# A two-block transformer forward pass on one core: early norms, a shorter forget-gate chain, and a last norm that starts tile by tile

## Chip, cores and metric

One core of one Trainium2 chip runs the whole forward pass. The metric is the device time of an execution in microseconds (us). Lower is better.

## What is computed

Two models run one after the other on one sequence of 512 tokens with 1024 channels. The parts that the change touches are these:

```python
def first_block(x, ...):
    for layer in range(2):
        h = rmsnorm(x, norm_mix[layer])
        x = x + (even_mixer if layer % 2 == 0 else odd_mixer)(h, ...)
        x = x + squared_relu_mlp(rmsnorm(x, norm_mlp[layer]), w_up[layer], w_down[layer])
    return rmsnorm(x, norm_final)

def even_mixer(h, w_in, b_forget, rel_bias, w_out):
    qa, ka, va, fa, qb, kb, vb = _split(h @ w_in, SPLIT_AB)        # fa: 8 columns, one per head
    log_f = jax.nn.log_sigmoid((fa + b_forget).astype(jnp.float32))
    o_a = fox_attention(qa, ka, va, log_f)      # scores + cumsum(log_f)[q] - cumsum(log_f)[k], causal
    o_b = chunked_relpos_attention(qb, kb, vb, rel_bias)
    return jnp.concatenate([o_a, o_b], -1) @ w_out

def second_block(x, ...):
    u = rms_norm(x, attn_norm_g)
    h = x + ((mg[0] * (y_a @ w_branch_a) + mg[1] * (y_b @ w_branch_b)) @ w_out)
    h = h + (jax.nn.silu(u2 @ w_gate) * (u2 @ w_up)) @ w_down      # u2 = rms_norm(h, ffn_norm_g)
    return rms_norm(h, final_norm_g)
```

## The kernel before

Activations lie transposed: channels on the 128 partitions, the 512 tokens along the free axis, so `x` is 8 tiles of 128x512. Every weight comes as a slab of 128x1024 floats (eight 128x128 tiles). A product keeps close to float32 by being three products: each operand is split into a rounded part (`hi`) and the rest (`lo`), and TensorE (PE) adds hi·hi, hi·lo and lo·hi (`product`, L458 to L467), 24 matmuls of 128x512 for a slab. ScalarE (ACT) rounds a slab in two halves (`split`, L1033), GpSimd (POOL) subtracts to get its low part (L440), and SyncE (SP) loads the next slab (L425) when a slot is free. There are two slots of raw, high and low weights and two or three PSUM banks for results; VectorE (DVE) takes results out and signals `gemm_free`.

Each engine has its own program, in an order written out by hand. Semaphores tie them together. An engine that waits holds back all that stands behind it. Four places matter here.

**The start.** ACT loads half of `x`, then for each tile j writes `h_hi` (L1064: x times the norm's gain, rounded) and the square of x (L1051, in two buffers `sq`). DVE writes `h_lo` (L1531) and adds the square to `acc` (L1524), tile by tile, in turn. PE, for each tile, makes three products of 8 columns for the forget gates (L497) and then three products of the first slab, v of pair 0. After tile 7, PE sums the squares over partitions with a matrix of ones (`norm_sum`, L489), DVE makes the mean, ACT makes 1/sqrt by Ln and Exp (`rsqrt`, L1058 and L1059), and only then can results be scaled.

**The gate chain.** With the scale known, DVE scales the 8 rows of forget logits (L1711), ACT makes ln(1+exp(-|z|)) (L1172 to L1174), and DVE adds, scans, splits into high and low, places the parts at four partition ranges of `turned`, and multiplies by four one-hot columns into `fox_b`, four tiles of 128x512 (L1714 to L1727). Behind these on DVE stand the low parts of q and k of pair 0 (L1639). Step 0 of the 32 attention steps (`scores`, L571 and L577) needs them all. Between them PE works on further slabs (`products`), 30 tiles ahead of step 0.

**The merge.** For the eight output tiles of the second model's mixer, DVE makes `m_hi` and `m_lo` (L2151 to L2153). The output projection (`project_out`, eight slabs) starts with one wait for all eight:

```python
            pe.wait_ge(act_lo, c.lo.at(8))
            c.lo.now += 8
            project_out(m_hi, m_lo)
```

**The end.** The last slab's result is added to x (L1569), squared (L1051), added to `acc` (L1524), summed by PE (L489), turned into a mean by DVE (L1561) and into `rstd` by ACT (L1058, L1059). Then DVE multiplies tile by tile by gain and rstd (L1539), and ACT issues one store of 256 KB after each (L1476).

## Time and profile before

| | |
|---|---|
| median of 3 runs | 2142.93 us (2142.56 to 2143.94) |
| the profiled execution | 2140.77 us |
| its span, first to last instruction | 2139.0 us |
| mean granted TensorE clock | 0.985 of full speed |
| busy: PE / DVE / ACT / POOL | 95% / 47% / 42% / 41% |
| HBM traffic | 83 GB/s over the span |

Read it as a kernel in which PE is busy nearly all the time, so that time is lost where PE stands still or runs at the lower clock, and at the two ends, where PE has nothing to do yet or any more. Starts are in us from the span's start. A matmul's listed duration contains its pipeline; what one costs in a row of them is the distance between two starts.

### The profile page before, as it was taken

How to read it: one execution, taken by the hardware profiler on the slowest of the kernel's cores; microseconds unless marked ns; L12 is line 12 of the kernel's file. 1: busy time of each engine (PE TensorE's matmuls, PEld its weight loads, DVE VectorE, ACT ScalarE, POOL GpSimd, SP SyncE). 2: the span in 40 equal slices, each digit the busy share in tenths (PEclk: the TensorE clock that was granted, in tenths of full speed). 3: DMA queues.
4: the chain of work that ended last, by engine and by line, in shares of the span. 5: the costliest groups of instructions: out<-in, count | busy, mean ns of one | idle time of the engine just before them, and what ended most of it. 6: DMA issues, size and time to landing. Idle time of an engine off the chain costs nothing. (4 is left out here: it accounts for less than half of the span.)

```text
span 2139.0 us, 28743 instructions
## 1 busy us (share of the span) xinstructions
PE 2036.3 (95%) x9992; PEld 1614.6 (75%) x9992; DVE 999.0 (47%) x1603; ACT 908.8 (42%) x1773; POOL 871.6 (41%) x648
## 2 busy tenths in 40 slices
PE   7999999999999978899999998998999999999997
PEld 5777688888887755688888886766667878888885
DVE  6445545322355677542312265777564553323134
ACT  4555543333343664442323355655554233223233
POOL 3223345444454221244444453542113545545454
PEclk9999999999999999999999999999999999999998
DMA  4222122222222110122222221321112222232223
GB/s 142 71 70 79 60 98 96 93 97 98 98 99 80 59 40 30 41 97 92 97 98 98 98 92 66 99 89 41 39 40 69 96 82 92 96 99 99 99 95 103
DMA packets 50614, 177.89 MB, mean 83 GB/s; under 512 B 5568, under 2 KB 5832, under 8 KB 50512
## 3 DMA queue, kind: packets, MB, share of 16 engines
q1 hardware_dynamic: 47536, 171.02, 24.2%
q10 hardware_dynamic: 2976, 5.48, 0.8%
q8 instruction: 68, 1.11, 0.2%
q14 instruction: 34, 0.28, 0.0%
HBM read 174.36 MB, written 2.12 MB: 83 GB/s over the span
## 5 line engine op out<-in xcount | busy, mean ns | idle before, releaser
L440 POOL TENSOR_TENSOR w_lo<-raw,w_hi 128x512 fp32r<-128x512 f32 x644 | 871.4, 1375 | 1247.9 <-ACT w_hi L1033 1247.7
L1033 ACT ACTIVATE w_hi<-raw 128x512 fp32r<-128x512 f32 x644 | 371.0, 624 | 844.4 <-PE gemm_banks L467 826.3
L465 PE MATMUL gemm_banks<-h_hi,w_hi 128*128 128x512 f32 x1512 | 614.6, 406 | 7.0 <-POOL w_lo L440 6.8
L467 PE MATMUL gemm_banks<-h_hi,w_lo 128*128 128x512 f32 x1512 | 593.4, 392 | 0.0
L466 PE MATMUL gemm_banks<-h_lo,w_hi 128*128 128x512 f32 x1512 | 593.1, 392 | 0.0
L465 PEld LDWEIGHTS gemm_banks<-h_hi,w_hi 128*128 128x128 f32 x1512 | 284.9, 188 | 89.3 <-issue 28.4
L465 PE MATMUL gemm_banks<-u_hi,w_hi 128*128 128x512 f32 x848 | 330.5, 390 | 4.2 <-POOL w_lo L440 2.9
L467 PEld LDWEIGHTS gemm_banks<-h_hi,w_lo 128*128 128x128 f32 x1512 | 284.8, 188 | 62.4
L466 PE MATMUL gemm_banks<-u_lo,w_hi 128*128 128x512 f32 x848 | 330.1, 389 | 0.0
L467 PE MATMUL gemm_banks<-u_hi,w_lo 128*128 128x512 f32 x848 | 330.1, 389 | 0.0
L466 PEld LDWEIGHTS gemm_banks<-h_lo,w_hi 128*128 128x128 f32 x1512 | 285.4, 189 | 57.0 <-issue 2.6
L1569 DVE TENSOR_TENSOR x<-gemm_banks,x 128x512 f32<-128x512 f32 x112 | 77.4, 691 | 316.8 <-PE gemm_banks L467 314.7
L465 PEld LDWEIGHTS gemm_banks<-u_hi,w_hi 128*128 128x128 f32 x848 | 159.2, 188 | 38.9 <-issue 3.7
L467 PEld LDWEIGHTS gemm_banks<-u_hi,w_lo 128*128 128x128 f32 x848 | 159.2, 188 | 33.1
L466 PEld LDWEIGHTS gemm_banks<-u_lo,w_hi 128*128 128x128 f32 x848 | 159.3, 188 | 32.8
L1770 DVE TENSOR_TENSOR u_lo<-tmp,u_hi 128x512 fp32r<-128x512 f32 x86 | 108.7, 1264 | 126.0 <-ACT u_hi L1224 109.0
L1142 ACT ACTIVATE probs<-score_banks,top 128x128 f32<-128x128 f32 (+3 forms) x192 | 99.4, 523 | 133.5 <-DVE top L1672 122.0
L1150 ACT ACTIVATE probs<-probs,share 128x128 f32<-128x128 f32 (+3 forms) x160 | 81.1, 554 | 75.1 <-DVE share L1694 36.6
L1505 DVE TENSOR_TENSOR tmp<-gemm_banks,rstd 128x512 f32<-128x512 f32 x52 | 36.0, 692 | 147.2 <-PE gemm_banks L467 145.9
L1762 DVE SCALAR_TENSOR_TENSOR tmp<-gemm_banks,rstd 128x512 f32<-128x512 f32 x64 | 44.3, 692 | 120.8 <-PE gemm_banks L467 118.0
L1524 DVE TENSOR_TENSOR acc<-acc,sq 128x512 f32<-128x512 f32 x59 | 78.6, 1333 | 10.8 <-ACT sq L1051 10.1
L1672 DVE CUSTOM_DVE_ANT_0 score_banks<-score_banks,sin 128x128 f32<-128x128 f32 (+3 forms) x96 | 45.3, 514 | 36.2 <-PE score_banks L920 36.1
(307 smaller groups left out, 1943.3 us busy)
## 6 DMA issues: line engine op xcount, KB each, us to landing
raw<-slabs SPq DMA_DIRECT2D x322, 512.0 KB, 3.2
table<-rel_rows ACTq DMA_DIRECT2D x4, 512.0 KB, 3.9
y_t<-x ACTq DMA_DIRECT2D x8, 256.0 KB, 2.1
x<-x_t SPq DMA_DIRECT2D x4, 256.0 KB, 6.6
x<-x_t ACTq DMA_DIRECT2D x4, 256.0 KB, 7.2
cos<-pos SPq DMA_DIRECT2D x2, 256.0 KB, 9.5
consts<-consts_packed SPq DMA_DIRECT2D x1, 452.5 KB, 8.2
params<-params_packed ACTq DMA_DIRECT2D x1, 211.5 KB, 4.3
```

The costliest lines, as they stand in the source:

```text
L440: pool.tensor_tensor(w_lo[:, j, part], raw[:, j, part], w_hi[:, j, part].bitcast(F32), ALU.subtract).then_inc(slab_split, 1)
L465: pe.matmul(out, high, rhs_hi, start=first, stop=False)
L466: pe.matmul(out, high, rhs_lo, start=False, stop=False)
L467: return pe.matmul(out, low, rhs_hi, start=False, stop=last)
L1033: act.activation(w_hi[:, m % 2, part], raw[:, m % 2, part], ACT.Copy).then_inc(slab_hi, 1)
L1142: act.activation(probs[:, b, head, 0:w], SC[:, 2 * b + head, 0:w], ACT.Exp, bias=top[:, b, head:head + 1], scale=-1.0, accum_out=mass[:, b ...
L1150: act.activation(probs[:, b, head, 0:w], probs[:, b, head, 0:w], ACT.Copy, scale=share[:, b, head:head + 1]).then_inc(evened, 1)
L1524: dve.tensor_tensor(sums[:, :], sums[:, :], sq[:, c.acc.slot, :], ALU.add).then_inc(acc_ready, 1)
L1569: dve.tensor_tensor(x[:, j, :], bank, x[:, j, :], ALU.add).then_inc(gemm_free, 1)
L1672: last = dve.tensor_tensor_reduce(z, z, masks[head], -1.0, 3e38, ALU.add, ALU.min, top[:, b, head:head + 1])
L1762: dve.scalar_tensor_tensor(tmp[:, s, :], result(), 0.0, rstd[:, :], ALU.max, ALU.mult).then_inc(gemm_free, 1)
L1770: dve.tensor_tensor(u_lo[:, j, :], tmp[:, 2 + s, :], u_hi[:, j, :].bitcast(F32), ALU.subtract).then_inc(act_lo, 1)
```

## The change

The squares of the input go into eight tiles of `g_b` (idle at that time), one each, and ACT makes all eight `h_hi` first. PE runs five products of zeros while it waits for the first tile. The forget gates take two products for a tile of x, not three: one with 40 columns (8 high, 24 zero, 8 low) and one with 8, all after the first slab. The sum of squares is asked of PE two tiles into the next slab. The gate chain is shorter: sigma is made from a Relu and the Ln, the scan takes both, ones times one-hot (128x128) replaces the four wide `fox_b`, and the mask and the one-hot tiles are made ahead of the scan. V of pair 0 is turned during k, not q. The lambda, bias-row and identity tables move into attention steps 0 to 2. The output projection's first slab waits tile by tile. At the end, the sum of squares is made in two parts, ACT reads the sum from PSUM, x times gain is made beside the slabs, DVE multiplies in six pieces, and SP and ACT issue a store each in turn.

```diff
@@ units
-                if (name == "q" and j == TURN_AT) or (name == "q1" and j == 1):
+                if (name == ("q" if p else "k") and j == TURN_AT and n == KT) or (name == "q1" and j == 1):
                     yield "vt", p, 0, 0
...
+FINAL = [(0, 1), (1, 2), (2, 4), (4, 6), (6, 7), (7, 8)]
@@ sync
+            for n in range(0, len(FINAL), 2):
+                sp.wait_ge(y_ready, n + 1)
+                sp.dma_start(y_rows(y_out, n), x[:, slice(*FINAL[n]), :]).then_inc(y_stored, 16)
@@ tensor
-            pe.wait_ge(forget_split, 2)
+            pe.wait_ge(zeros_ready, 1)
+            for n in range(5):
+                pe.matmul(SC[:, 0, :], turned[:, 0, 0:P], turned[:, 0, :], start=True, stop=True)
             for kt in range(KT):
                 pe.wait_ge(act_lo, c.lo.at(kt + 1))
-                for n, (w, h) in enumerate(((wf_hi, h_hi), (wf_hi, h_lo), (wf_lo, h_hi))):
-                    last = pe.matmul(OB[0:8, :], w[:, kt, :], h[:, kt, :], start=(kt == 0 and n == 0), ...
...
+            for kt in range(KT):
+                pe.matmul(OB[0:40, :], wf[:, kt, :], h_hi[:, kt, :], start=kt == 0, stop=False, ...
+                last = pe.matmul(OB[0:8, :], wf[:, kt, 0:8], h_lo[:, kt, :], start=False, stop=kt == KT - 1, ...
             pe.wait_ge(small_landed, 16)
-            norm_sum(KT, bank=0)
...
-            products(KT, AB_AHEAD)
+            products(KT, KT + 2)
+            norm_sum(KT, bank=0)
+            products(KT + 2, AB_AHEAD)
...
-            pe.wait_ge(act_lo, c.lo.at(8))
-            c.lo.now += 8
-            project_out(m_hi, m_lo)
+            gemm_slab(m_hi, m_lo, fresh=1)
+            for n in range(1, KT):
+                gemm_slab(m_hi, m_lo)
...
-            norm_sum(KT)
+            pe.wait_ge(acc_ready, c.acc.at(KT - 1))
+            pe.matmul(OB[:, :], ones, acc[:, :], start=True, stop=False)
+            pe.wait_ge(sq_ready, c.acc.at(KT))
+            pe.matmul(OB[:, :], ones, sq[:, (c.acc.now + KT - 1) % 2, :], start=False, stop=True).then_inc(norm_full, 1)
@@ scalar
                 gained(j, gains_of("mix0"))
-                square(x[:, j, :])
-                if j == 5:
+            for j in range(KT):
+                if j == 4:
                     split(1)
+                act.activation(g_b[:, j, :], x[:, j, :], ACT.Square).then_inc(sq_ready, 1)
...
             products(0, KT)
+            rsqrt(rstd)
...
+            act.activation(tmp[0:8, 3, :], tmp[0:8, 2, :], ACT.Relu, bias=small[0:8, 4:5], scale=-1.0)
...
+            products(KT, 2 * KT)
+            act.wait_ge(fox_ready, 5)
+            act.activation(fox[64:72, :], tmp[0:8, 2, :], ACT.Copy).then_inc(fox_hi, 1)
...
                     if finish:
                         act.wait_ge(gemm_free, c.gemm.at())
                         square(x[:, j, :])
+                        act.activation(g_b[:, j, :], x[:, j, :], ACT.Copy,
+                                       scale=gains_of("final2")[:, j:j + 1]).then_inc(gained_out, 1)
...
-            rsqrt(rstd)
+            link(act.activation(rstd[:, :], OB[:, :], ACT.Ln, bias=small[:, 5:6], scale=1.0 / D))
+            act.activation(rstd[:, :], rstd[:, :], ACT.Exp, scale=-0.5).then_inc(rstd_ready, 1)
@@ vector
-            mean(D, rstd)
-            g = PC["final2"].start
-            for j in range(KT):
-                normed(x[:, j, :], params[:, g + j:g + j + 1], x[:, j, :], rstd)
+            dve.wait_ge(rstd_ready, c.rstd.at(1))
+            dve.wait_ge(gained_out, KT)
+            for low, high in FINAL:
+                dve.tensor_tensor(x[:, low:high, :], g_b[:, low:high, :],
+                                  rstd[:, :].unsqueeze(1).to_broadcast([P, high - low, S]), ALU.mult).then_inc(y_ready, 1)
```

How the order moves, at the three places the prediction speaks of. First PE at the start of the program, before (`wf` are the forget weights, `out_bank` their PSUM bank):

```order
L497 MATMUL out_bank<-h_hi,wf_hi 8x512 [waits act_lo,forget_split]
L497 MATMUL out_bank<-h_lo,wf_hi 8x512
L497 MATMUL out_bank<-h_hi,wf_lo 8x512
L465 MATMUL gemm_banks<-h_hi,w_hi 128x512 [waits slab_split]
L466 MATMUL gemm_banks<-h_lo,w_hi 128x512
L467 MATMUL gemm_banks<-h_hi,w_lo 128x512
```

and now:

```order
L512 MATMUL score_banks<-turned 128x512 [waits zeros_ready]
L512 MATMUL score_banks<-turned 128x512 x4
L482 MATMUL gemm_banks<-h_hi,w_hi 128x512 [waits slab_split,act_lo]
L483 MATMUL gemm_banks<-h_lo,w_hi 128x512
L484 MATMUL gemm_banks<-h_hi,w_lo 128x512
L482 MATMUL gemm_banks<-h_hi,w_hi 128x512 [waits act_lo]
```

The forget products have gone from between the tiles and stand, two for a tile, behind the slab's 24 products. The five products of zeros wait for a memset only.

Second, DVE from the last `h_lo` to the scan and the low parts of q and k, before:

```order
L1531 SCALAR_TENSOR_TENSOR h_lo<-x,params,h_hi 128x512 [waits act_hi]
L1524 TENSOR_TENSOR acc<-acc,sq 128x512 [waits acc_ready,sq_ready]
L1619 TENSOR_SCALAR ident_r<-consts 128x128 [waits small_landed]
```

and now:

```order
L1574 SCALAR_TENSOR_TENSOR h_lo<-x,params,h_hi 128x512 [waits act_hi] x8
L1669 TENSOR_TENSOR acc<-g_b 128x512 [waits sq_ready]
L1669 TENSOR_TENSOR acc<-acc,g_b 128x512 [waits acc_ready,sq_ready] x6
L1673 COPY tmp<-out_bank 8x512 [waits forget_full]
L1674 TENSOR_TENSOR tmp<-tmp,out_bank 8x512 [waits dve_step]
L1604 TENSOR_SCALAR rstd<-score_banks 128x512 [waits norm_full,dve_step]
L1752 TENSOR_TENSOR tmp<-tmp,rstd 8x512 [waits rstd_ready]
```

All eight `h_lo` now come ahead of all seven additions, and the tables (three masks, lambda) that stood between the additions and the mean are gone from here; `PE` asks for the sum of squares after 6 products of the next slab.

Third, PE at the output projection, before:

```order
L465 MATMUL gemm_banks<-m_hi,w_hi 128x512 [waits slab_split,gemm_free,act_lo]
L466 MATMUL gemm_banks<-m_lo,w_hi 128x512
L467 MATMUL gemm_banks<-m_hi,w_lo 128x512
L465 MATMUL gemm_banks<-m_hi,w_hi 128x512
L466 MATMUL gemm_banks<-m_lo,w_hi 128x512
```

and now:

```order
L482 MATMUL gemm_banks<-m_hi,w_hi 128x512 [waits act_lo,slab_split,gemm_free]
L483 MATMUL gemm_banks<-m_lo,w_hi 128x512
L484 MATMUL gemm_banks<-m_hi,w_lo 128x512
L482 MATMUL gemm_banks<-m_hi,w_hi 128x512 [waits act_lo]
L483 MATMUL gemm_banks<-m_lo,w_hi 128x512
```

The products stand where they stood; each of the eight tiles now waits for its own `act_lo`, where the first waited for the count of all eight.

## Rows read from the trace of the kernel before

**Rows 1.** PE's waits over the whole span: total us, times, longest
```profile
PE gemm_banks L465 <- POOL w_lo L440: 9.8, 5, 4.3
PE out_bank L497 <- DVE h_lo L1531: 8.9, 1, 8.9
PE score_banks L571 <- DVE k_lo L1639: 4.9, 1, 4.9
PE gemm_banks L465 <- DVE m_lo L2153: 4.7, 1, 4.7
```
**Rows 2.** Timeline, PE at the start and at the first sum of squares
```profile
10.16 0.63 PE L465 MATMUL gemm_banks<-h_hi,w_hi 128*128 128x512 f32 x1
...
14.23 0.39 PE L497 MATMUL out_bank<-h_lo,wf_hi 128*8 128x512 f32 x1
14.46 0.39 PE L497 MATMUL out_bank<-h_hi,wf_lo 128*8 128x512 f32 x1
...
22.23 1.02 PE L489 MATMUL score_banks<-acc,consts 128*128 128x512 f32 x2
```
**Rows 3.** Timeline, ACT and DVE, first input tiles
```profile
6.50 0.72 ACT L1064 ACTIVATE h_hi<-x,params 128x512 fp32r<-128x512 f32 x1 [0.32 <-DMA x<-x_t]
7.13 0.61 ACT L1051 ACTIVATE sq<-x 128x512 f32<-128x512 f32 x1
...
7.26 1.52 DVE L1531 SCALAR_TENSOR_TENSOR h_lo<-x,params,h_hi 128x512 fp32r<-128x512 f32 x1 [1.61 <-ACT h_hi L1064]
```
**Rows 4.** Timeline, DVE and POOL meeting in SBUF
```profile
14.76 0.69 DVE L1524 TENSOR_TENSOR acc<-acc,sq 128x512 f32<-128x512 f32 x1
15.36 1.79 DVE L1531 SCALAR_TENSOR_TENSOR h_lo<-x,params,h_hi 128x512 fp32r<-128x512 f32 x1
...
14.17 4.13 POOL L440 TENSOR_TENSOR w_lo<-raw,w_hi 128x512 fp32r<-128x512 f32 x2 [5.94 <-ACT w_hi L1033]
25.98 2.53 POOL L440 TENSOR_TENSOR w_lo<-raw,w_hi 128x512 fp32r<-128x512 f32 x2 [7.69 <-ACT w_hi L1033]
```
**Rows 5.** Timeline, PE at attention step 0 and after it
```profile
43.62 0.48 PE L571 MATMUL score_banks<-fox_b,ones_r 64*128 64x128 f32 x2 [4.90 <-DVE k_lo L1639]
...
44.67 0.79 PE L465 MATMUL gemm_banks<-h_hi,w_hi 128*128 128x512 f32 x1
...
48.20 0.40 PE L467 MATMUL gemm_banks<-h_hi,w_lo 128*128 128x512 f32 x1
```
**Rows 6.** Timeline, PE, DVE and POOL at the output projection
```profile
1711.67 2.93 POOL L440 TENSOR_TENSOR w_lo<-raw,w_hi 128x512 fp32r<-128x512 f32 x2 [2.89 <-ACT w_hi L1033]
...
1714.92 0.69 DVE L2153 TENSOR_TENSOR m_lo<-tmp,m_hi 128x512 fp32r<-128x512 f32 x1
1715.67 0.80 PE L465 MATMUL gemm_banks<-m_hi,w_hi 128*128 128x512 f32 x1 [4.74 <-DVE m_lo L2153]
...
1720.83 0.40 PE L465 MATMUL gemm_banks<-m_hi,w_hi 128*128 128x512 f32 x1
1721.06 0.40 PE L466 MATMUL gemm_banks<-m_lo,w_hi 128*128 128x512 f32 x1
```
**Rows 7.** Timeline, the last norm and the stores
```profile
2124.97 0.63 ACT L1051 ACTIVATE sq<-x 128x512 f32<-128x512 f32 x1 [3.45 <-DVE x L1569]
...
2126.43 1.70 PE L489 MATMUL out_bank<-acc,consts 128*128 128x512 f32 x2 [2.23 <-DVE acc L1524]
2128.17 0.69 DVE L1561 TENSOR_SCALAR rstd<-out_bank 128x512 f32<-128x512 f32 x1 [1.79 <-PE out_bank L489]
...
2130.22 6.26 DVE L1539 SCALAR_TENSOR_TENSOR x<-x,params,rstd 128x512 f32<-128x512 f32 x8 [1.36 <-ACT rstd L1059]
2131.00 5.85 ACTq L1476 DMA_DIRECT2D y_t<-x  x8
```
**Rows 8.** Stretches of 1 us: PEclk, DMA share and GB/s are the last three
```profile
10.00:11.00 1.00, 1.00 (x3) 0.73 (x3) 1.00 (x3) 1.00 (x3) 0.00 (x0) 1.00 1.07 428
...
2133.00:2134.00 1.00, 0.00 (x0) 0.00 (x0) 0.96 (x2) 0.00 (x0) 0.00 (x0) 0.50 0.94 344
```

More of the change, by code:

```diff
@@ L273, in e_valued, with y_rows @@
     return 128 + (s if s <= DIFF_STEPS else 2 * s - DIFF_STEPS)
+FINAL = [(0, 1), (1, 2), (2, 4), (4, 6), (6, 7), (7, 8)]
+def y_rows(y_out, n):
+    low, high = FINAL[n]
+    return y_out[low * P:high * P, :].rearrange("(j p) s -> p j s", p=P)
 def build(nc, slabs, x_in, params_in, consts_in, pos1_in, pos2_in, rel_in, lam_in, y_out):
@@ L507, in _ @@
             c.lo.now += KT
+            pe.wait_ge(forget_split, 3)
+            for kt in range(KT):
+                pe.matmul(OB[0:40, :], wf[:, kt, :], h_hi[:, kt, :], start=kt == 0, stop=False, skip_group_check=True)
+                last = pe.matmul(OB[0:8, :], wf[:, kt, 0:8], h_lo[:, kt, :], start=False, stop=kt == KT - 1,
+                                 skip_group_check=True)
+            last.then_inc(forget_full, 1)
             pe.wait_ge(small_landed, 16)
-            norm_sum(KT, bank=0)
-            pe.wait_ge(masks_ready, 3)
             used, done = {}, {}
@@ L1113, in _ @@
                 gained(j, gains_of("mix0"))
-                square(x[:, j, :])
-                if j == 5:
+            for j in range(KT):
+                if j == 4:
                     split(1)
-            act.wait_ge(lam_in_ready, 1)
-            act.activation(small[:, 2:4], small[:, 0:2], ACT.Exp).then_inc(lam_exp, 1)
-            rsqrt(rstd)
+                act.activation(g_b[:, j, :], x[:, j, :], ACT.Square).then_inc(sq_ready, 1)
+            c.acc.now += KT
             def products(low, high):
@@ L1187, in _ @@
                 products(*half(s, 1))
+                if s == 1:
+                    act.wait_ge(lam_in_ready, 1)
+                    act.activation(small[:, 2:4], small[:, 0:2], ACT.Exp).then_inc(lam_exp, 1)
+                    act.wait_ge(rel_ready, 3)
+                    act.dma_start(rel_rows, table[0:8, 1, :, :].rearrange("p a b -> p (a b)")[:, 0:E_LEN]).then_inc(
+                        rel_stored, 16)
             mixed(7)
@@ L1564, in mean, with add_out @@
                 c.rstd.now += 1
-            def add_out(gains=None, beside=lambda j: None, more=False, squares=True):
+            def add_out(gains=None, beside=lambda j: None, more=False, squares=True, last_apart=False):
                 for j in range(KT):
@@ L1572, in add_out @@
                         gained(j, gains)
-                    if squares:
+                    if squares and (j < KT - 1 or not last_apart):
                         add_square(j == 0)
@@ L1620, in _ @@
-            dve.tensor_tensor(gain2[:, :], gains_of("final1"), gains_of("attn2"), ALU.mult)
-            lam = VT[:, 0:256].rearrange("p (a b d) -> p a b d", a=2, b=2)
-            dve.wait_ge(pos_landed, 48)
-            prods = VT[:, 256:384].rearrange("p (a d) -> p a d", a=2)
-            link(dve.tensor_tensor(prods, lam[:, :, 0, :], lam[:, :, 1, :], ALU.mult))
-            dve.tensor_reduce(small[:, 0:2], prods, X, ALU.add).then_inc(lam_in_ready, 1)
-            dve.wait_ge(lam_exp, 1)
-            link(dve.scalar_tensor_tensor(neg_lam[:, :], small[:, 3:4], -LAM_INIT, small[:, 2:3], ALU.add,
-                                          ALU.subtract))
+            for j in range(1, KT):
+                dve.wait_ge(sq_ready, j + 1)
+                if j > 1:
+                    dve.wait_ge(acc_ready, j)
+                dve.tensor_tensor(acc[:, :], (acc if j > 1 else g_b[:, 0, :])[:, :], g_b[:, j, :],
+                                  ALU.add).then_inc(acc_ready, 2 if j == 1 else 1)
@@ L1632, in _ @@
+            c.acc.now += KT
+            dve.wait_ge(forget_full, 1)
+            link(dve.tensor_copy(tmp[0:8, 3, :], OB[32:40, :]))
+            link(dve.tensor_tensor(tmp[0:8, 2, :], tmp[0:8, 3, :], OB[0:8, :], ALU.add))
             mean(D, rstd, 0)
@@ L1754, in _ @@
                 bias_table(s)
+                if s == 0:
+                    tables_begun()
+                if s == 2:
+                    dve.wait_ge(lam_exp, 1)
+                    dve.scalar_tensor_tensor(neg_lam[:, :], small[:, 3:4], -LAM_INIT, small[:, 2:3], ALU.add, ALU.subtract)
+                    for name, tile in (("ident", ident_r), ("strict", strict_r)):
+                        dve.tensor_scalar(tile[:, :], consts[:, CO[name]], 1.0, None, ALU.mult).then_inc(masks_ready, 1)
+                    dve.tensor_tensor(gain2[:, :], gains_of("final1"), gains_of("attn2"), ALU.mult)
             mixed(7)
```

110 lines of the change are left out of this document (59 added, 51 removed).

## The prediction

> **What bounds the kernel now.** The page's first part says PE is busy 95% of the span, so I read PE's waits next. Nearly all of them are short waits in the attention stages, which the change leaves alone. Three are touched: 8.9 us before the first product, 4.9 us ahead of attention step 0, and 4.7 us ahead of the output projection [rows 1]. The fourth place is the end, where PE is done and a chain of single operations and stores runs [rows 7]. The largest sum in the list, POOL's 9.8 us in five waits [rows 1], is at other slabs; the first of them in time lies far behind step 0, and no edit reaches it.
>
> A wait costs more than its length. Behind the wait of 4.74 us, 12 products of 128x512 take 5.16 us (1715.67 to 1720.83), 0.43 us each, and then they stand 0.23 us apart [rows 6]: the clock at 1.2 and at 2.4 GHz. The same two paces are seen at the start, where a product's listed 0.63 us becomes 0.39 and the distance 0.23 (14.23 to 14.46) [rows 2], and behind the wait of 4.9 us, up to about 48 us [rows 5].
>
> **The start.** Before, PE does 48 products and one sum between 8.9 and 22.7, and starts step 0 at 43.62 [rows 2, 5]. I put the new program through the rows' durations.
>
> - PE: five float32 products of zeros from about 1.5 us. One of these, in two passes, costs 1.70 us at the low clock [rows 7] and about 0.9 at the high one (its two passes are listed with 1.02, of which the last 0.1 or so overlaps with what follows) [rows 2]. Two and a half slow, the rest fast: done near 8, ahead of the first tile. So they cost nothing, and leave PE at 2.4 GHz when tile 0 comes.
> - Tile 0's `h_lo` ends at 8.78, as before [rows 3]. ACT's `h_hi` now follow each other at some 0.62 us (start of L1064 to start of L1051, 6.50 to 7.13), so DVE sends tiles faster than PE takes them (3 x 0.23 = 0.69 us). The slab ends at 8.85 + 8 x 0.69 = 14.4; the 16 forget products make it 14.4 + 16 x 0.23 = 18.1. Before, slab and forget products ended at 22.2. That is 4.1 us won so far, 1.8 of it from 8 products fewer, and 2.3 from the clock and the pace.
> - Then 6 products, to 19.4, and PE wants the squares' sum. Here the change gives back. DVE adds only after the last `h_lo`, from 13.1 us, and that is when POOL takes two slabs in a row (ACT rounds slab 1 from about 13.6 and slab 2 from about 16.8). Where both work on SBUF, a DVE operation of 0.69 takes 1.79 and POOL's pair 4.13 and not 2.53 [rows 4]: they go one at a time, in turn. Seven additions alone are 7 x 0.62 = 4.3 us, so 17.5; in turn with four POOL operations of 1.25 I get 21 to 22.3. PE waits 2 to 3 us. The clock may drop once more here (it was down after 2.23 us of idling at the end [rows 7]).
> - From the sum at 22.3: 0.9, then 18 products of q (4.1), 24 of k and the turning of V (6.0), 6 of v1 x 3 ahead of step 0 (4.1): PE arrives at 37.4. DVE's chain for step 0 is beside that: mean and rsqrt to 25.8, scaled logits 26.5, four ACT operations to 29.2, the scan to 30.6, and then what is late now is the pair of fox low parts and k_lo, which again meet POOL's next slab: 38 to 38.7. I take **38.0**.
>
> Gain at step 0: 43.6 - 38.0 = 5.6. The wait there shrinks from 4.9 to about 1 us, so the slow stretch behind it goes: 44.67 to 48.20 for 8 distances [rows 5] is 3.5 us where 8 x 0.23 = 1.8, and the eight small score products before it lose half of 1.05: 2.1 us. The start brings **7.7 us**, between 5 (a second drop of the clock at 19.4) and 10 (the additions slip between POOL's operations, step 0 at 36).
>
> The tables moved into steps 0 to 2 are a dozen small operations, under 2 us of DVE in all and one ACT issue, in stretches where both wait for PE. Cost 0; without that cover, at most 2 us. Relu, the copy of 8 rows and the negated bias are in the chain above.
>
> **The output projection.** `m_lo` of tile 7 ends at 1715.6 whatever PE does [rows 6]. PE is free at 1710.8 (4.74 us before 1715.67). Tiles 0 to 6 are 21 products at the 0.233 us of this stage (1720.83 to 1721.06) [rows 6], 4.9 us: PE reaches tile 7 at 1715.7, just when it is there. Won: 4.9 us of waiting, and the 12 slow products, 1715.67 to 1720.83 = 5.16 us for 12 x 0.233 = 2.8, so 2.4. Together **7.2 us**. What comes next is slab 1, asked for at 1716.4; POOL has it at 1714.6 [rows 6]. Bounds 6.5 and 7.4.
>
> **The end.** Before: square ends 2125.6, addition, sum 2126.43 to 2128.1 at the low clock, mean, Ln, Exp, first multiply at 2130.22, first store issued at 2131.00 [rows 7]. Now the sum over seven squares is done while x is added and squared, so PE's gap is 0.7 us and not 2.2, and I expect the high clock: last square 2125.6, sum 2126.5, Ln and Exp (1.36 from the mean's end to the first multiply, with hand-overs) 2127.9, first piece 2128.6, issue 2128.7. That is 2.3 us sooner (addition 0.7, mean 0.7, clock 0.8, the rest hand-overs). The product with the gain on ACT (0.72 for a tile) has 2 to 3 us of idling before it, and the last one ends before the sum does.
>
> Will the stores keep up? Eight stores go out 0.79 us apart [rows 7], and the 16 DMA engines are 94% busy at 344 GB/s [rows 8]. So they, not DVE, nearly set the pace already; DVE's pieces at about 0.6 us a tile only fill the last 6%: 2.1 MB at 365 GB/s instead of 344 is 0.35 us. At the start both queues together moved 428 GB/s [rows 8], though reading HBM. If two issuing queues brought that rate here, 2.1 MB would take 4.9 us for 6.1, 1.2 us won and not 0.35. I take 0.35, since this row is of the same direction. The Trainium skill (DMA: Bandwidth & Descriptors, on issuing engines and queues) says that SP and ACT queues share the same 16 engines and a second one saves issue time only; by it the sum stays at 0.35, and no run so far shows stores on two queues. The end brings **2.7 us**, between 1.5 (the sum at the low clock) and 4.
>
> **The sum.** 7.7 + 7.2 + 2.7 = 17.6 us. On the profiled execution's 2140.77 that is 2123.2; its time is 2.2 below the median of the runs, 2142.93, and the forecast is for a median: **2125.3 us**. The three places are in line on PE, so their gains add. A measurement of this kernel can tell some 0.2% (4.3 us) from no change.
>
> **Rivals.**
>
> - *The additions slip through* (chance 0.14). POOL let two DVE operations in a row pass before at 14 us [rows 4]. With the squares done by 20 us PE hardly waits, step 0 starts at 36, and with full DMA rate at the end the sum is 10 + 7.3 + 3.7 = 21: 2122. Against it: four POOL operations now fall into the seven additions.
> - *The clock* (0.18). The products of zeros end early, or the wait for the squares drops the clock again. Eight tiles at 0.43 us a product would end the slab 3 to 4 us later, of which the wait for the squares hides most; a drop at 19.4 costs up to 12 slow products, 2.3 us; the sum at the end at the low clock 0.8. Then 5 + 7.2 + 1.6 = 13.8: 2129. For it: the same 4.7 us wait and the 2.2 us one both ended in a slow stretch. The Trainium skill (TensorE: Matmul & The Clock Gate, Part 1) says that the number of slow products at a start varies from run to run; by that rule this case and the forecast may alternate between runs of one kernel. The runs before differ by 1.4 us in all.
> - *The projection's tile waits do nothing* (0.04): were the first product to wait for all eight tiles still, as the order of semaphore counts could make it, 7.2 us are missing: 2132.5. The order shows separate waits, so this is small.
> - *Slower* (0.01). The clock, once up on products of zeros and idle again, stays low through the first attention steps. Each product of 128x512 at 1.2 GHz costs 0.2 us more [rows 2], so 17.6 us are used up after 88 such products, and 110 (13 tiles of 8 short) would give 2147. The trace speaks against it: the slow stretches behind both waits ended, the longer after 12 products [rows 5, 6].
>
> The rest, 0.63, is my forecast, with 2122.5 to 2128 as its own range.
>
> **How the numbers follow.** The range should reach the first two rivals: from 2121 to 2130 only the projection's failure and worse are outside. Faster by over 0.2% needs under 2138.6: all cases but the last, 0.97. Within 0.2%: 0.02. Slower: 0.01.
>
> **What would show it.** Step by step: PE's first slab product at about 8.9 with 0.23 us distances; a wait of 2 to 3 us for `acc` near 19.4; step 0 at 38; no wait ahead of the projection, and its tile 7 within 0.3 us of `m_lo`; the last sum in about 0.9 us, the first store near 2128.7 less 15 (about 2114), and a DMA share near 1 behind it. The forecast is wrong if the first slab's products stand 0.42 us apart, if step 0's wait for k_lo stays at several us, or if a wait of over 1 us appears in attention steps 0 to 3, where the tables went.

## The result, and the profile after

| | before | after |
|---|---|---|
| median of the runs, us | 2143.24 (5 runs) | 2131.32 (5 runs, 2129.74 to 2131.77) |
| profiled execution, us | 2140.77 | 2129.74 |
| its span, us | 2139.0 | 2127.9 |

The ratio of after to before is 0.9948, 95% interval 0.9937 to 0.9959: 11.1 us faster by the ratio, 11.9 by the medians. The forecast was 2125.3 us, with a range of 2121 to 2130. The time lies outside the range, 6.0 us above the forecast: of 17.6 us expected, 11.9 came (11.0 between the two profiled executions). Lines of the kernel after stand 17 to 43 further down: the three products are now L482 to L484, POOL's subtraction L457, `norm_sum` L506, the scores L592 and L598.

**The three places.** First the start. The timeline of PE in the kernel after (start us, duration, engine, line, operation, tiles, and in brackets the idle time ahead of it and what ended it):

```profile
1.46 7.50 PE L512 MATMUL score_banks<-turned 128*128 128x512 f32 x10 [1.46 <-DVE turned L1650]
8.79 0.50 PE L482 MATMUL gemm_banks<-h_hi,w_hi 128*128 128x512 f32 x1
...
14.41 0.39 PE L526 MATMUL out_bank<-h_hi,wf 128*40 128x512 f32 x1
...
17.87 0.39 PE L527 MATMUL out_bank<-h_lo,wf 128*8 128x512 f32 x1
...
22.44 1.13 PE L506 MATMUL score_banks<-acc,consts 128*128 128x512 f32 x2 [2.79 <-DVE acc L1669]
```

and DVE and POOL beside it:

```profile
14.08 8.30 DVE L1669 TENSOR_TENSOR acc<-acc,g_b 128x512 f32<-128x512 f32 x6
...
14.69 3.00 POOL L457 TENSOR_TENSOR w_lo<-raw,w_hi 128x512 fp32r<-128x512 f32 x2 [6.49 <-ACT w_hi L1061]
18.46 3.38 POOL L457 TENSOR_TENSOR w_lo<-raw,w_hi 128x512 fp32r<-128x512 f32 x2 [0.77 <-ACT w_hi L1061]
```

The six additions take 8.30 us, 1.38 each, where the first, ahead of POOL's slabs, took 0.68: the two engines go in turn, as in [rows 4]. PE waits 2.79 us for them. Then step 0, which stood at 43.62 with a wait of 4.90 [rows 5]:

```profile
38.90 0.33 PE L592 MATMUL score_banks<-fox,fox_of 64*128 64x128 f32 x2 [1.23 <-DVE k_lo L1682]
...
39.49 0.50 PE L482 MATMUL gemm_banks<-h_hi,w_hi 128*128 128x512 f32 x1
39.83 0.40 PE L483 MATMUL gemm_banks<-h_lo,w_hi 128*128 128x512 f32 x1
```

At the output projection no wait is left ahead of the first `m_hi` product, where 4.74 us stood [rows 6]. PE reaches tile 7 (1714.04) when its `m_lo` has just been written; the distance behind that product is 0.34 us (1714.04 to 1714.38), the others stay at 0.23:

```profile
1709.08 0.40 PE L482 MATMUL gemm_banks<-m_hi,w_hi 128*128 128x512 f32 x1
...
1714.04 0.50 PE L482 MATMUL gemm_banks<-m_hi,w_hi 128*128 128x512 f32 x1
1714.38 0.39 PE L483 MATMUL gemm_banks<-m_lo,w_hi 128*128 128x512 f32 x1
```

The end, all engines:

```profile
2115.26 1.02 PE L1043 MATMUL out_bank<-acc,consts 128*128 128x512 f32 x2
...
2116.86 1.12 PE L1045 MATMUL out_bank<-sq,consts 128*128 128x512 f32 x2 [0.59 <-ACT sq L1079]
2118.09 0.69 ACT L1514 ACTIVATE rstd<-out_bank,small 128x512 f32<-128x512 f32 x1 [0.66 <-PE out_bank L1045]
...
2119.52 4.77 DVE L2239 TENSOR_TENSOR x<-g_b,rstd 128x512 f32<-128x512 f32 x6 [3.37 <-ACT rstd L1515]
2120.24 3.81 SPq L444 DMA_DIRECT2D y_t<-x  x3
2120.85 3.83 ACTq L1519 DMA_DIRECT2D y_t<-x  x3
```

From the last square to the first store it was 6.03 us (2124.97 to 2131.00) [rows 7]; now it is 2120.24 - 2116.18 = 4.06, with the square starting at 2116.18. Two stretches of 1 us behind that (columns as in [rows 8]) show the store rate late in the tail, about 380 GB/s where 344 stood. Over the whole tail, from the first store's issue to the end of the span, it is 7.7 us (2120.24 to 2127.9) where 8.0 stood (2131.00 to 2139.0):

```profile
2124.00:2125.00 1.00, 0.00 (x0) 0.00 (x0) 0.29 (x1) 0.00 (x0) 0.00 (x0) 0.50 1.02 387
2125.00:2126.00 1.00, 0.00 (x0) 0.00 (x0) 0.00 (x0) 0.00 (x0) 0.00 (x0) 0.50 1.02 383
```

**So where are the missing microseconds?** I laid the two traces side by side: the same instruction on DVE, its start before minus its start after. These are worked out from the two traces, in us (the first column is the time in the kernel before):

```
at 74.89    (attention 1 has settled)     +6.81
at 684.7    (end of the first MLP)        +6.85
at 718                                    +4.8
at 815                                    +5.1
at 871                                    +4.0
at 1316                                   +3.6
at 1564                                   +3.4
at 1577.75  (late in attention 3)         +1.69
at 1723.90  (behind output projection)    +8.78
at 2124.24  (last x)                      +8.79
end of the span                          +11.0
```

The start brought 6.8, the projection 7.1, the end 2.3: 16.2 us. But in attention stages two and three, between 684 and 1578, 5.1 us went again, though the change was meant to leave them alone. The largest groups of PE's waits are nearly what they were. Before (three groups of the attention stages that [rows 1] leaves out, each larger than its 9.8 us):

```profile
PE score_banks L760 <- ACT probs L1292: 15.5, 8, 3.7
PE out_bank L966 <- DVE turned L2087: 13.0, 11, 3.7
PE out_bank L774 <- DVE turned L1879: 11.7, 15, 2.2
```

and after:

```profile
PE score_banks L783 <- ACT probs L1328: 15.5, 8, 3.7
PE out_bank L990 <- DVE turned L2145: 12.7, 11, 3.7
PE out_bank L797 <- DVE turned L1937: 11.1, 13, 2.4
PE gemm_banks L482 <- POOL w_lo L457: 10.1, 6, 4.3
```

One wait did grow, and by the change's own doing. The new condition in `units` (V of pair 0 is turned during k and not q) holds for stage two as well. There too V's turning moved, and DVE now copies V right ahead of what `k_lo` needs. Before:

```profile
676.61 0.69 DVE L1839 COPY V<-gemm_banks 128x512 f32<-128x512 f32 x1
...
688.06 0.33 PE L750 MATMUL score_banks<-k_hi,q_hi 64*128 64x128 f32 x2 [1.68 <-DVE k_lo L1821]
```

and after:

```profile
679.01 0.69 DVE L1897 COPY V<-gemm_banks 128x512 f32<-128x512 f32 x1
...
681.95 0.33 PE L773 MATMUL score_banks<-k_hi,q_hi 64*128 64x128 f32 x2 [2.33 <-DVE k_lo L1879]
```

PE waits 0.65 us longer there. The wait is 2.33 us in all four profiles with the new start and no fill products (those come below), and 1.7 in all four with the old one. So some 0.7 of the 5.1 us is no matter of the clock.

For the rest, what differs is the granted clock. In that stretch, 11 pieces of the trace after are at 0.50, together 54.6 us; in the trace before it was 37.5 us in 7 pieces. All of them start during a wait of PE or just behind one. For instance the one that begins with the wait of 4.3 us for `w_lo` (stretches; PEclk, DMA share and GB/s are the last three):

```profile
1290.00:1294.00 4.00, 1.70 (x8) 1.09 (x6) 2.12 (x4) 1.81 (x4) 0.00 (x0) 1.00 0.00 0
1294.00:1304.00 10.00, 6.53 (x17) 4.88 (x18) 3.84 (x6) 4.68 (x8) 5.01 (x4) 0.51 0.14 52
1304.00:1308.00 4.00, 4.00 (x20) 2.94 (x19) 0.75 (x2) 0.89 (x2) 0.17 (x1) 0.94 0.43 131
```

and its first products, at 0.43 us instead of 0.23:

```profile
1295.98 0.77 PE L482 MATMUL gemm_banks<-h_hi,w_hi 128*128 128x512 f32 x1 [4.28 <-POOL w_lo L457]
1296.55 0.63 PE L483 MATMUL gemm_banks<-h_lo,w_hi 128*128 128x512 f32 x1
1296.97 0.63 PE L484 MATMUL gemm_banks<-h_hi,w_lo 128*128 128x512 f32 x1
```

Theory A: what was lost is TensorE's clock in stages two and three, whose low stretches fall differently in each execution. Theory B: the change itself does something to those stages. Rival C: the low clock there is harmless, because the engine that PE waits for sets the time. (Each expectation below letters its own theories anew.)

### The profile page after: what moved, and what is told of

It is laid out like the page before. It is cut to its first block and busy times, and to the rows that moved or that the text cites. A ratio compares the mean times of both kernels' runs of the same rounds, so it can differ in the third digit from the quotient of the medians.

```text
span 2127.9 us, 28756 instructions
## 1 busy us (share of the span) xinstructions
PE 2043.0 (96%) x9996; PEld 1619.3 (76%) x9996; DVE 999.3 (47%) x1600; ACT 915.1 (43%) x1783; POOL 871.1 (41%) x648
## 5 line engine op out<-in xcount | busy, mean ns | idle before, releaser
L457 POOL TENSOR_TENSOR w_lo<-raw,w_hi 128x512 fp32r<-128x512 f32 x644 | 870.9, 1373 | 1239.7 <-ACT w_hi L1061 1239.5
L482 PE MATMUL gemm_banks<-h_hi,w_hi 128*128 128x512 f32 x1512 | 615.4, 407 | 7.4 <-POOL w_lo L457 7.2
L484 PE MATMUL gemm_banks<-h_hi,w_lo 128*128 128x512 f32 x1512 | 593.7, 393 | 0.0
L482 PEld LDWEIGHTS gemm_banks<-h_hi,w_hi 128*128 128x128 f32 x1512 | 285.1, 189 | 89.6 <-issue 28.2
L482 PE MATMUL gemm_banks<-u_hi,w_hi 128*128 128x512 f32 x848 | 330.3, 390 | 4.1 <-POOL w_lo L457 2.9
L484 PEld LDWEIGHTS gemm_banks<-h_hi,w_lo 128*128 128x128 f32 x1512 | 285.2, 189 | 62.9
L484 PE MATMUL gemm_banks<-u_hi,w_lo 128*128 128x512 f32 x848 | 329.9, 389 | 0.0
L482 PEld LDWEIGHTS gemm_banks<-u_hi,w_hi 128*128 128x128 f32 x848 | 159.2, 188 | 38.8 <-issue 3.7
L484 PEld LDWEIGHTS gemm_banks<-u_hi,w_lo 128*128 128x128 f32 x848 | 159.2, 188 | 33.2
L1567 DVE TENSOR_TENSOR acc<-acc,sq 128x512 f32<-128x512 f32 x51 | 71.0, 1391 | 10.1 <-ACT sq L1079 9.3
```

The lines of the kernel that those rows point to most:

```text
L457: pool.tensor_tensor(w_lo[:, j, part], raw[:, j, part], w_hi[:, j, part].bitcast(F32), ALU.subtract).then_inc(slab_split, 1)
L482: pe.matmul(out, high, rhs_hi, start=first, stop=False)
L484: return pe.matmul(out, low, rhs_hi, start=False, stop=last)
L1567: dve.tensor_tensor(sums[:, :], sums[:, :], sq[:, c.acc.slot, :], ALU.add).then_inc(acc_ready, 1)
```

## The experiments

Medians are of all runs of a kernel; the kernel before ran beside each set, and its median was 2142.51, 2141.97 and 2142.10 in the three.

### Set 1: the change in parts, and each kernel profiled again

**The new start alone.** The change without the projection's tile-wise wait and without the new end:

```diff
-            gemm_slab(m_hi, m_lo, fresh=1)
-            for n in range(1, KT):
-                gemm_slab(m_hi, m_lo)
+            pe.wait_ge(act_lo, c.lo.at(8))
+            c.lo.now += 8
+            project_out(m_hi, m_lo)
...
```

> The changed kernel with the old output projection wait and the old end: only the start and the attention steps 0 to 2 are changed. Theory A (each part is worth what its place shows, and the stages between are as they were): 6.9 us faster than before, as at the end of the first attention stage. Theory B (the part is worth that, but the stages between lose part of it because other waits there end at the lower clock): 1.5 to 4 us faster, and the profile shows more low-clock stretches between 600 and 1700 us than the seven of the kernel before. Theory C (the moved tables or the changed buffers slow the stages themselves): the same loss as B, but with longer waits and the same number of low stretches.

Measured: 2138.71 us (2135.83 to 2143.64, 10 runs), ratio 0.9986 (0.9976 to 0.9995): 3.0 us faster by the ratio, 3.8 by the medians. The executions of this one program lie 7.8 us apart. Its profiled execution had a low stretch that the trace after does not have, behind the wait for `acc`:

```profile
22.65 1.72 PE L492 MATMUL score_banks<-acc,consts 128*128 128x512 f32 x2 [2.75 <-DVE acc L1644]
23.38 1.42 PE L468 MATMUL gemm_banks<-h_hi,w_hi 128*128 128x512 f32 x1
24.60 0.63 PE L469 MATMUL gemm_banks<-h_lo,w_hi 128*128 128x512 f32 x1
```

It cost 2.1 us (the gain at 74.89 is 4.73 and not 6.81), and 5.1 more went in the stages, with 10 low stretches there where the kernel before has 7. That is what its theory B named, time and stretches; the 6.9 us of its theory A did not come.

**Everything but the new start.** The kernel before with the projection and the end of the change:

```diff
-            pe.wait_ge(act_lo, c.lo.at(8))
-            c.lo.now += 8
-            project_out(m_hi, m_lo)
+            gemm_slab(m_hi, m_lo, fresh=1)
+            for n in range(1, KT):
+                gemm_slab(m_hi, m_lo)
...
-            norm_sum(KT)
+            pe.wait_ge(acc_ready, c.acc.at(KT - 1))
+            pe.matmul(OB[:, :], ones, acc[:, :], start=True, stop=False)
...
```

> The kernel before with the tile-by-tile output projection and the new end alone. All that comes ahead of the merge is untouched, so all theories expect the stages between as before, and a gain of 7.1 at the projection and 2.3 at the end: 9.4 us faster. If it is well under 9, the low stretch behind the projection's wait was not there in most executions, and the profile of before overstates it.

Measured: 2131.26 us (2130.63 to 2134.01, 4 runs), ratio 0.9947 (0.993 to 0.9963): 11.3 us faster, more than expected and as fast as the whole change. Its profiled execution, the slowest of the four (2134.01), lost 3.6 us in the stages, with the old start. That speaks against theory B in its simplest form: no new start is needed for such a loss. But this execution is 2.75 us above the median of its kernel, and its stages lost nothing at the two places that go with the new start (the longer wait for `k_lo` above, and one at 1566 that is named further down).

**The two kernels again,** unchanged:

> The changed kernel once more, for a second profile. If the low-clock stretches depend on how the program lies in time to something outside it, they stand at other waits than in the first profile and their number differs by one to four. If they are the program's own, they stand at the same eleven places.

> The kernel before once more, for a second profile: the same question. If the stretches are the program's own: again nine between 40 and 1722 us at the same waits. If not: other places, and a time that differs with their number, about 1 us for each.

Measured: 2130.14 and 2142.07. The second profile of the kernel after lost 5.1 us in the stages once more, with 10 of the 11 low stretches at the same waits; only the one at 1321 is missing. So they are mostly the program's own. The second profile of the kernel before differs from the first by up to 1.6 us in mid-program (+1.54 at 813, -1.45 at 1533). Six of its seven stretches in the stages stand behind the same waits again; the one at 689.8 to 693.3 is missing, and a piece at 868.1 to 871.5 and one at 1325.5 to 1328.9 are new. Same program, same waits, mostly the same stretches, and some that come and go.

### Set 2: the clock held up

> The changed kernel itself, timed again beside the three others of this set. Theory A (each execution lays the stretches of low granted clock in the long middle stages anew, and the kernel after met more of them): median 2129 to 2133, and the stretches near 683, 707, 765, 806, 864, 1294, 1321, 1407, 1479, 1523 and 1567 us come back at about the same places, because the same waits stand ahead of them. Theory B (the 5.1 us that were lost between 684 and 1576 us were an accident of one execution): some executions near 2125 to 2127.

Measured: 2129.27 us (2126.30 to 2130.58, 5 runs), ratio 0.9942 (0.9929 to 0.9956). The profiled execution lost 3.3 us in the stages; low stretches lie near 683, 765, 1294, 1403, 1475, 1519 and 1564 again, one near 792 is new, and those at 707, 806, 864 and 1321 are missing. The places mostly come back, and one execution of five, 2126.30, also lies where the other theory put some: the loss is neither wholly fixed nor a single accident; part of it is drawn anew in each execution.

**Fill products.** Products of zeros ahead of the waits behind which the clock was low, each group shorter than its wait (135 products of 128x512 in all, more than the estimate in the expectation):

```diff
+FILL_CD_FLIP = {2: 6, 6: 5, 10: 12, 11: 3, 13: 4, 14: 7, 15: 7}
+FILL_CD_VALUES = {15: 7, 18: 4, 22: 4, 26: 7}
+FILL_E_SLAB = {("kc", 0): 13, ("k", 1): 6}
+FILL_E_FLIP = {36: 5}
+FILL_E_VALUES = {9: 10, 18: 11, 27: 10, 37: 3}
...
+            def fill(n, to=None):
+                for _ in range(n):
+                    pe.matmul(OB[:, :] if to is None else to, zero_r[:, :], zero_r[:, :].unsqueeze(1)...)
...
                 p, i, b, w = block_of(s)
+                fill(FILL_CD_FLIP.get(s, 0))
                 pe.wait_ge(evened, cd_evened(s))
```

In this form they write zeros over finished columns of the attention output's bank, so later values are others than the reference's; every instruction of the kernel still runs.

> The changed kernel with products of zeros on PE ahead of the fifteen or so waits after which the clock was low (attention stages two and three, about 115 products of 0.227 us = 26 us, each group shorter than the wait that it stands in). Theory A: the clock stays at 2.4 GHz there, the low time of 54 us falls under 20, and since PE's products take 0.43 instead of 0.227 us in it, 4 to 15 us come back: 2116 to 2127. Theory B (the low clock does not matter, because the engine that is waited for sets the time): 2130 to 2133. Theory C (the fill products hold up PE more than the clock gives): over 2133.

Measured: 2119.11 us (2118.10 to 2121.32, 4 runs), ratio 0.9899 (0.9883 to 0.9914): 10.2 us faster than the kernel after beside it (2129.27). Between 684 and 1578 no low stretch is left. This is the number of that expectation's theory A; its B (the low clock does not matter, rival C above) and its C fall.

> The kernel before with the same fill products at the same places. Theory A (the parts of the change add where the clock in the stages between is the same for both): it is slower than the filled changed kernel by 15 to 17 us (6.8 at the start, 7.1 at the projection, 2.3 at the end, as the profiled executions gave them), where the kernels without fill products differ by 11.9. Theory B (what was lost between is not the clock but something that the change does to the stages): the two filled kernels differ by 11 to 13 us again.

Measured: 2131.88 us (2130.77 to 2132.07, 5 runs), ratio 0.9955 (0.9942 to 0.9969): 10.1 us faster than the kernel before. So in the medians the fill products gave both kernels the same, some 10 us. The two filled kernels differ by 12.8 us, 2 to 4 less than theory A expected and inside what B expected. The traces say where it is short: the start of the filled changed kernel again had a low stretch, at 23.6 to 27.0, and had gained 4.7 us at 74.89, not 6.8. The wait for `k_lo` at the start of stage two is still there in it (0.7 us behind the fill products) and not in the filled kernel before, and the projection's wait in the filled kernel before was followed by a shorter low stretch (1706.3 to 1709.7), so that 6.4 us lie between the two there and not 7.1. Only the next set could tell the two theories apart.

```profile
22.71 1.26 PE L519 MATMUL score_banks<-acc,consts 128*128 128x512 f32 x2 [2.75 <-DVE acc L1692]
23.27 1.13 PE L490 MATMUL gemm_banks<-h_hi,w_hi 128*128 128x512 f32 x1
24.20 0.63 PE L491 MATMUL gemm_banks<-h_lo,w_hi 128*128 128x512 f32 x1
```

**The projection alone** (the first diff hunk of the run without the new start, on the kernel before):

> The kernel before with the output projection waiting tile by tile, and nothing else. By the profiled executions the projection gave 7.1 us of its own: 2135 to 2136.5. If the start only re-deals the clock, this part keeps its whole gain, and with the end's 2.3 it explains most of what the run without the new start gained (11.3). Rival (low clock behind the projection's start comes back in another place): under 5 us, 2137.5 or more.

Measured: 2133.72 us (2133.27 to 2136.71, 6 runs), ratio 0.9965 (0.9953 to 0.9977): 7.5 us by the ratio, 8.3 by the medians, 1.3 us better than the expected range. The profiled execution gained 7.05 behind the projection and had lost nothing in the stages (-0.03 at 1577.75); its low stretches there are the seven of the first profile of before, at the same times to 0.4 us.

### Set 3: held clock, and each part undone

The fill products now go only into columns of the bank in which no value stands yet, so nothing is overwritten, and eight more stand in the start:

```diff
+            def fill(n, to=None, low=0):
+                to, open_ = (OB[:, low:S], True) if to is None else (to, False)
+                for _ in range(4 * n * P // (S - low)):
+                    pe.matmul(to, zero_r[:, :], zero_r[:, :].unsqueeze(1).to_broadcast([P, (S - low) // P, P]), ...)
...
             products(KT, KT + 2)
+            pe.wait_ge(zeros_ready, 2)
+            fill(8, SC[:, 0, :])
             norm_sum(KT, bank=0)
```

> The changed kernel with the fill products of the run before (now only into columns of the bank that no value stands in), and eight more of them in the start, ahead of PE's wait for acc, behind which a stretch of low clock lay in two of the profiled executions with the new start (23.0 to 26.5 us in one, 23.6 to 27.0 in the other). Theory A (the clock is what is lost, in the start too): the start keeps its whole gain, against 4.4 at 48 us in the filled run, so 2116 to 2118.5, with no low stretch before the last products. Theory B (the start's loss was something else): 2119 again.

Measured: 2118.07 us (2117.69 to 2119.18, 4 runs), ratio 0.9892 (0.9876 to 0.9909). It leaves nothing out, and beats both kernels: 24.0 us faster than before, 11 to 13 faster than the change. Its page, and the pieces of its timeline that answer to those above:

```profile
PE   9999999999999989999999999999999999999997
...
PEclk9999999999999999999999999999999999999999
```

```profile
19.69 1.99 PE L514 MATMUL score_banks<-zero_r 128*128 128x512 f32 x8
22.67 1.13 PE L521 MATMUL score_banks<-acc,consts 128*128 128x512 f32 x2 [0.99 <-DVE acc L1696]
...
23.86 0.39 PE L491 MATMUL gemm_banks<-h_lo,w_hi 128*128 128x512 f32 x1
...
1287.30 3.13 PE L514 MATMUL gemm_banks<-zero_r 128*128 128x512 f32 x13
1291.64 0.50 PE L490 MATMUL gemm_banks<-h_hi,w_hi 128*128 128x512 f32 x1 [1.21 <-POOL w_lo L465]
1291.98 0.39 PE L491 MATMUL gemm_banks<-h_lo,w_hi 128*128 128x512 f32 x1
```

```profile
1289.00:1299.00 10.00, 6.89 (x32) 5.12 (x31) 4.55 (x7) 4.82 (x8) 5.05 (x4) 1.00 0.16 54
```

The thirteen fill products take 3.13 us of the wait for `w_lo`; `w_lo` lands no sooner, but the products behind it stand 0.23 us apart and not 0.43. The stretch of 10 us is at clock 1.00, where the kernel after had 0.51. The only low stretch left in the trace is the one behind the last products. The fill is not free: groups that may use only 128 or 256 columns of the bank cost more for their columns (28 of 128 columns, as many columns as 7 of 512, take 3.24 us, and the 7 of 512 take 1.77), and likely for that, between 783 and 813 this kernel won 0.7 us where the run before won 1.7.

Now each part of the change is undone in this kernel. First the start (the fill products of the start go with it):

> The run best with the start of the kernel before (its own low stretch at 41 to 48 us is left in). Theory A, gains add when the clock between is held: slower than best by 6.5 to 7.3 us. Rival (the start's gain is given back in the stages whatever the clock does): by under 5.

Measured: 2124.37 us (2123.10 to 2125.55, 4 runs): 6.3 slower than best. In the two traces it is 7.05 us at 74.89 (6.57 and -0.48) and 5.95 at 1577.75: of the 1.1 between, 0.7 is the wait for `k_lo` at the start of stage two, which the old `units` takes away.

Then the projection:

> The run best with the output projection waiting for all tiles at once, as before. Theory A: slower than best by 6.4 to 7.3 us (4.9 of wait and about 2.2 of low clock behind it). Rival: only the wait counts, 4.9 or less, if the clock stays high behind it in most executions.

Measured: 2125.31 us (2124.03 to 2128.63, 4 runs): 7.2 slower.

Then the end:

> The run best with the end of the kernel before (last square in acc, normalisation and stores tile by tile on one queue). Theory A: slower than best by 2.3 to 2.7 us, what the profiled executions and the prediction gave. Rival (the end's gain is larger in the median than in the profiled executions): 3.5 or more.

Measured: 2119.94 us (2119.55 to 2121.25, 4 runs): 1.9 slower.

The projection lies inside what theory A expected, the start 0.2 and the end 0.4 us below it; the rivals of all three (under 5, 4.9 or less, 3.5 or more) fall. Together 15.4 us. For all kernels the gains over the first trace of before, at the same landmarks (us, from one profiled execution each):

```
                  at 74.89  1577.75  1723.90  2124.24  between 74.89 and 1577.75
after                6.81     1.69     8.78     8.79      -5.1
after, again         6.45     1.31     8.42     8.41      -5.1
after, timed again   6.52     3.26    10.35    10.35      -3.3
new start only       4.73    -0.33     0.36     0.34      -5.1
no new start         1.01    -2.62     4.50     4.51      -3.6
projection only      0.11    -0.03     7.05     7.04      -0.1
before, again       -0.61    -1.28    -1.06    -1.05      -0.7
before, filled       0.53     9.77    10.46    10.45      +9.2
after, filled        4.74    13.32    20.41    20.43      +8.6
best                 6.57    13.68    20.50    20.48      +7.1
best, old start     -0.48     7.73    12.97    12.97      +8.2
best, old proj.      6.56    13.82    13.22    13.22      +7.3
best, old end        6.54    13.77    20.65    20.63      +7.2
```

The last column scatters by 5 us in the seven executions without fill products, and by 2 in the six with them. The seven divide by their start. Three of the four with the new start lost 5.1 us and one 3.3; the three with the old start lost 0.1, 0.7 and 3.6. Two places make most of that. One is the wait for `k_lo`, 0.7 us. The other is in late stage three. The product group ahead of it starts after a shorter wait with the new start (0.51 us for 0.79), and PE waits longer at this one; before, and after:

```profile
1569.11 0.88 PE L929 MATMUL score_banks<-consts,probs 128*128 128x128 f32 x6 [1.38 <-ACT probs L1150]
```

```profile
1565.85 0.87 PE L953 MATMUL score_banks<-consts,probs 128*128 128x128 f32 x6 [1.66 <-ACT probs L1175]
```

The wait is 1.66 us in all four with the new start, and a low stretch stands behind it in all four (1567.3 to 1570.7 in the first), which costs 1.6 us in three and 3.2 in the one timed again. It is 1.38 us in all four traces with the old start (the first of before included), and none has a low stretch there or loses anything. Together that is 2.3 us, or 3.9 in the one timed again, that went with the new start each time. What is left, 2.8 us to a gain of 0.6, overlaps with the 0 to 3.6 of the old start, and of that the draw can be the cause.

## Why the prediction was wrong

**What held.** Each place did what the sum said. The products of zeros ended at 8.96, free, and left the clock high; the first slab product came at 8.79 (8.85 expected), the slab ended at 14.4 (14.4), the forget products at 18.1 (18.1). PE waited 2.79 us for `acc` (2 to 3), whose additions went in turn with POOL, and the sum came at 22.44 (22.3). Step 0 came at 38.90 (38.0; 38 to 38.7 was the spread I gave): the fox low parts and `k_lo` stand in DVE's queue until 38.84. The low stretch behind it went, as expected. The tables in steps 0 to 2 cost nothing that shows: no wait of over 1 us there. At the projection 7.2 was expected and 7.1 measured (the sum counts 4.9 us of waiting where its own row has 4.74), by the trace, by the run alone (7.05 in its trace) and by undoing it (7.2). At the end the first store came 2.0 us sooner and the tail behind it was 0.3 shorter, 2.3 for 2.7; the 0.35 for the stores was about right.

**Sizes.** The start was worth 6.8 and not 7.7 (0.9 us, step 0's later start), the end 2.3 and not 2.7. With 0.1 at the projection those are 1.4 of the 6.5 us between the sum (2123.2 for the profiled execution) and its 2129.74.

**The step that failed** is the last one of the sum: "The three places are in line on PE, so their gains add." They are in line, and by the runs at held clock they add: 6.3 + 7.2 + 1.9 = 15.4 with each undone. But I treated the 1500 us between the first two places as a fixed length that is only shifted ("the attention stages, which the change leaves alone"). It is not. PE waits there some 20 times for 1 to 4 us, and behind such a wait the clock may be at 1.2 GHz or not. The first trace of before had 37.5 us of low clock in those stages, the trace after 54.6, and 5.1 us of the missing 6.5 went there. Of these, 0.7 is no clock but the longer wait for `k_lo`, which the change itself made; 1.6 is the low stretch at 1567, which came with the new start in four profiles of four and without it in none of four; the other 2.8 lie within what executions of the old start also lose (0 to 3.6). So the term that the sum put at nothing is the length of the stages between, and it held two things: a loss that goes with the change, and a scatter that a single execution of each kernel cannot show.

The medians say the same. Undone at held clock the parts give 15.4 us (the longer wait for `k_lo` is already in that, since best has it too), and the change gave 11.9 in its medians. So some 3.5 us more were lost to the clock than in the kernel before; a mere draw, the same for both kernels, would hardly show in medians, though those of best and its variants are of 4 runs each.

I had looked at the two waits that the change removes and seen the low clock behind both [rows 5, 6], and priced its going at 2.1 and 2.4 us. The same pricing applied to the other waits of [rows 1] and their neighbours would have shown that the kernel had 37.5 us of slow stretches elsewhere, and that these are a source both of scatter and of gain. But [rows 1] holds only four groups of waits, and the prediction calls POOL's 9.8 us the largest sum in that list, where the whole view has three larger ones, all in the attention stages.

**The rivals.** *The clock* (chance 0.18) named 2129, which is near the 2129.3 and 2131.3 of the two sets, but by other terms: it put the loss at the start and at the end, where the first profiled execution had none. Two of the five executions with the new start and without fill in it did have the drop it described, at 23.0 and 23.6, right behind the wait for `acc`, at a price of 2.1 us (it said up to 2.3). The Trainium skill (TensorE: Matmul & The Clock Gate, Part 1) says that the same kernel shows another number of slow products from run to run, depending on when its first product falls; by that rule I let the case alternate between runs at the start only. Such a stretch in two profiles of five is in line with the Trainium skill. That stretches also come and go behind waits in the middle of a kernel (at 707, 792, 806, 864 and 1321 in the three profiles of the kernel after) is what the runs add. *The additions slip through* did not occur: six additions took 1.38 us each. *The projection's tile waits do nothing* and *slower* are refuted.

**What stays open.** Why the clock falls at 1567 with the new start each time: the wait ahead of it is 0.28 us longer, and whether that is the cause was not tried. How the loss of the changed kernel's stages divides in the median: in the medians of set 2 filling gave both kernels 10 us, but the filled changed kernel's profile carries the low stretch at the start, which costs 2.1 us and which no profile of the kernel after has. By the traces filling gave its stages 12 to 14 us (from -5.1 and -3.3 to +8.6) and those of the kernel before 9 to 10. The runs without the new start (11.3 for an expected 9.4) and the projection alone (7.5 to 8.3 for 7.1) did better than their parts, and I have no cause for that. The new start alone did worse (3.0 to 3.8 for 6.8), with losses in its trace at 23.0 and, among others, at the two places above. That the whole scatter of a kernel comes from the clock was not shown; best's four runs lie 1.5 us apart, those of the new start alone 7.8.

## What to carry to other kernels

Gains at separate places add only if what lies between them has a fixed length: before you add, take the granted clock of the stages between from the trace, and count each wait of some 1.4 us or more on TensorE as one that may be followed by a stretch at half speed (1.37 us, at 1615.08 in best with the old start, is the shortest that was, here). Give a forecast the scatter of that as its width. Compare the orders of all engines over the whole program too: here one changed condition reached a stage that was thought untouched. And such waits are worth more than their length in a repair: products of zeros into columns that nobody uses, ahead of a wait and shorter than it, gave back 10 us (0.5%) here without shortening a single one of the things that were waited for.

## What the runs showed of the hardware that I had not expected

- Waits far shorter than those at the start suffice. In the first execution of the kernel after the clock fell behind waits of 1.9 us (706.78) and 2.2 us (862.78); in the one timed again it did not fall behind these two. The pieces that the trace after has and the one of before has not, at 707, 864 and 1567, took 1.1 to 1.6 us each off the gain.
- Products whose operands are all zeros hold the clock as real ones do, and pass as fast (8 of 128x512 in 1.99 us, the end of the last included).
- The stores from two queues moved 383 to 387 GB/s in the two stretches shown, with the DMA share at 1.0, where one queue fed tile by tile had 344 at 0.94 [rows 8]. The Trainium skill (DMA: Bandwidth & Descriptors, on issuing engines) says that a second queue saves issue time only. The trace does not speak against that: the rate stayed under the 428 GB/s that loads reached [rows 8], and the size of the stores and DVE's pace changed along with the queues, so no run here tells which of the three raised it.
